# Giving each buffer that TensorE reads its own offset within 512 bytes, in a two-block float32 network

## The reference

```
_swiglu_ffn:  g, u = split(x @ w_gate_up);  (silu(g) * u) @ w_down        width 1024 -> 2 x 2816 -> 1024
conv_ffn:     u = causal_dwconv(x @ w_up);  (silu(gate) * up) @ w_down    width 1024 -> 2 x 2816 -> 1024
block 1:      u @ w_in,  mixed @ w_out,  h @ w_ple_gate,  two feed-forward nets per layer
block 2:      hn @ w_in,  mix @ w_out,  rmsnorm(h) @ w_ple_gate,  one feed-forward net per layer
```

## Time and profile before

| | before |
|---|---|
| time, median of 2 runs | 3952.97 us |
| span of the profiled execution | 3950.6 us |
| TensorE matmul busy | 3812.4 us (97%), 17790 matmuls |
| TensorE weight loads busy | 3050.4 us (77%) |
| VectorE / ScalarE / GpSimd busy | 2334.5 / 1510.9 / 511.5 us |
| mean granted TensorE clock | 0.986 |
| HBM read | 307.94 MB, 78 GB/s over the span |

### The profile page before, as it was taken

How to read it: one execution, slowest core, us unless ns; L and a number is a source line. 1 busy time by engine, 2 the same in 40 slices (tenths; PEclk the granted TensorE clock), 3 DMA queues, 4 the chain that set the end, 5 groups by cost and what they waited for, 6 DMA issues and landing times. The chain is left out here.

```text
span 3950.6 us, 46607 instructions
## 1 busy us (share of the span) xinstructions
PE 3812.4 (97%) x17790; PEld 3050.4 (77%) x17790; DVE 2334.5 (59%) x3213; ACT 1510.9 (38%) x2188; POOL 511.5 (13%) x366
## 2 busy tenths in 40 slices
PE   8999989999999998999989999999999999999997
PEld 6888758888788885788877678788877767878886
DVE  5455766445544475744467675775567665675656
ACT  3224653223322365322243444343343353343333
POOL 1001731000100055100020013200010002220002
PEclk9999989999999999999999999999999999999999
DMA  4333203333233330233332100122233110022222
GB/s 152 96 96 112 66 21 96 96 96 111 86 98 99 97 106 11 79 100 96 96 114 80 49 22 1 43 96 96 96 109 107 59 38 6 12 80 96 96 96 80
DMA packets 87018, 314.99 MB, mean 80 GB/s; under 512 B 10016, under 2 KB 10400, under 8 KB 86176
## 3 DMA queue, kind: packets, MB, share of 16 engines
q1 hardware_dynamic: 83664, 302.43, 24.4%
q10 hardware_dynamic: 3152, 9.74, 0.7%
HBM read 307.94 MB, written 2.10 MB: 78 GB/s over the span
## 5 line engine op out<-in xcount | busy, mean ns | idle before, releaser
L384 ACT ACTIVATE wh<-raw 128x1024 fp32r<-128x1024 f32 x564 | 597.4, 1059 | 1630.3 <-PE ps L404 1317.5
L402 PE MATMUL ps<-xh,wh 128*128 128x512 f32 x2336 | 918.0, 393 | 16.7 <-DVE xl L467 10.0
L403 PE MATMUL ps<-xl,wh 128*128 128x512 f32 x2336 | 910.8, 390 | 0.0
L404 PE MATMUL ps<-xh,wl 128*128 128x512 f32 x2336 | 910.5, 390 | 0.0
L388 DVE TENSOR_TENSOR wl<-raw,wh 128x1024 fp32r<-128x1024 f32 x564 | 695.6, 1233 | 181.1 <-ACT wh L384 180.2
L402 PEld LDWEIGHTS ps<-xh,wh 128*128 128x128 f32 x2336 | 439.8, 188 | 112.4 <-issue 19.6
L403 PEld LDWEIGHTS ps<-xl,wh 128*128 128x128 f32 x2336 | 440.0, 188 | 94.3 <-issue 3.6
L404 PEld LDWEIGHTS ps<-xh,wl 128*128 128x128 f32 x2336 | 439.8, 188 | 91.9
L402 PE MATMUL ps<-fh,wh 128*128 128x512 f32 x1016 | 397.1, 391 | 4.0 <-DVE wl L388 4.0
L404 PE MATMUL ps<-fh,wl 128*128 128x512 f32 x1016 | 395.4, 389 | 0.0
L403 PE MATMUL ps<-fl,wh 128*128 128x512 f32 x1016 | 395.3, 389 | 0.0
(11 more groups left out here) (467 smaller groups left out, 5529.6 us busy)
## 6 DMA issues: line engine op xcount, KB each, us to landing
raw<-in_w SPq DMA_DIRECT2D x564, 512.0 KB, 3.5
con<-in_consts SPq DMA_DIRECT2D x1, 2053.5 KB, 14.0
h<-in_x SPq DMA_DIRECT2D x4, 512.0 KB, 6.9
p_t<-in_p ACTq DMA_DIRECT2D x4, 512.0 KB, 3.9
w1k<-in_w1c ACTq DMA_DIRECT2D x2, 1024.0 KB, 4.9
w1v<-in_w1c ACTq DMA_DIRECT2D x2, 1024.0 KB, 7.0
out<-h SPq DMA_DIRECT2D x8, 256.0 KB, 2.2
dup_k<-roped ACTq DMA_DIRECT2D x8, 128.0 KB, 3.6
```

Source lines behind the costliest of these rows:

```text
L384: nc.scalar.activation(wh[k % 2][:, :], raw[k % 4][:, :], ACT.Copy).then_inc(s["w_hi"], 1)
L402: nc.tensor.matmul(DB[k % 2][:, :], a, hi(q), start=(q == order[0]), stop=False)
L403: nc.tensor.matmul(DB[k % 2][:, :], a, lo(q), start=False, stop=False)
L404: last = nc.tensor.matmul(DB[k % 2][:, :], b, hi(q), start=False, stop=(q == order[-1]))
```

## The change

The allocator gets a method `phase`, which moves the next start up to a given offset within 512 bytes. The buffers that TensorE reads in the dense stages get the phases of the table above. The skipped bytes need room, and it comes from a smaller scratch area for dynamic DMAs (4096 bytes per partition in place of the default; the first free byte falls from 16481 to 4193, so the arena starts at 4224 in place of 16512, and both have phase 128). Tensors that share the place of `fh` in the mixing stages (`qkv`, `roped`, `p_hi`, `p_lo`, `diag`, `sp_b`, `stick`, `w1k`, `w1v`, the accumulators `acc1` and `acc2`) move with it from phase 128 to 256; constants, `gbuf`, `sq`, `e_t`, `h` and all others keep their phase. No instruction is added, removed or moved on any engine.

```diff
+LINE = 512
@@ class Layout
+    def phase(self, offset):
+        self.at += (offset - self.at) % LINE
+        return self
@@ build
-        x_at = sb.at
-        xh = sb("xh", [P, DC, T], F32R)
-        xl = sb("xl", [P, DC, T], F32R)
-        f_at = sb.at
+        x_at = sb.phase(128).at
+        xh = sb.phase(128)("xh", [P, DC, T], F32R)
+        xl = sb.phase(160)("xl", [P, DC, T], F32R)
+        f_at = sb.phase(256).at
         fh = sb("fh", [P, 8, T], F32R)
-        fl = sb("fl", [P, 8, T], F32R)
+        fl = sb.phase(320)("fl", [P, 8, T], F32R)
+        sb.phase(128)
         raw = [sb(f"raw{k}", [P, UW]) for k in range(4)]
-        wh = [sb(f"wh{k}", [P, UW], F32R) for k in range(2)]
-        wl = [sb(f"wl{k}", [P, UW], F32R) for k in range(2)]
-        con_at = sb.at
+        wh = [sb.phase((128, 448)[k])(f"wh{k}", [P, UW], F32R) for k in range(2)]
+        wl = [sb.phase((160, 384)[k])(f"wl{k}", [P, UW], F32R) for k in range(2)]
+        con_at = sb.phase(128).at
@@ block1, block2
-                gl_ = Layout(nc, m.at, 32768)
-                gh, gl = (gl_(f"gate1{n}", [P, DC, T], F32R) for n in ("hi", "lo"))
+                gl_ = Layout(nc, m.at, 34816)
+                gh, gl = (gl_.phase(k)(f"gate1{n}", [P, DC, T], F32R) for n, k in (("hi", 32), ("lo", 416)))
...
+                gh, gl = (gl_.phase(k)(f"gate2{n}", [P, DC, T], F32R) for n, k in (("hi", 96), ("lo", 288)))
@@ kernel
-    nc = _bacc.Bacc("TRN2", target_bir_lowering=False, num_devices=1)
+    nc = _bacc.Bacc("TRN2", target_bir_lowering=False, num_devices=1, dynamic_dma_scratch_size=4096)
```

More of the change, by code:

```diff
@@ L1364, in block2 @@
                 m.at += -(-4 * NS2 // 32) * 32
-                gl_ = Layout(nc, m.at, 32768)
-                gh, gl = (gl_(f"gate2{n}", [P, DC, T], F32R) for n in ("hi", "lo"))
+                gl_ = Layout(nc, m.at, 34816)
+                gh, gl = (gl_.phase(k)(f"gate2{n}", [P, DC, T], F32R) for n, k in (("hi", 96), ("lo", 288)))
                 small_end = m.at
```

## The result

The changed kernel took 4011.36 us (two runs, 4011.27 and 4011.44) against 3952.97, +58.4 us, which is 1.0148 by the two medians. The ratio on record is 1.0143, with a 95% interval of 1.0123 to 1.0163: under two per cent, but clear of the noise. The forecast was 3928, range 3870 to 3995. The slower rival had said 4005.

What follows compares the result with a forecast made beforehand. The prediction took TensorE's matmul pitch in the dense stages as the bound. Its terms, 8.4 - 25.2 - 7.8 = -24.6 us from 3952.97, gave 3928 us, range 3870 to 3995.

Steps and rivals of the forecast that it cites:

- slower rival: Odd x and all f units: any distance other than 0 costs 6.4 ns, +52 us, 4005 us (half price 3979); chance 0.25.
- What bounds: Dense stages: TensorE is the bound, so each nanosecond between two matmuls counts; one nanosecond on all is 13 us.
- The scratch, ScalarE, VectorE: 0.: Whole kernel: smaller DMA scratch costs 0, and ScalarE and VectorE work at other phases is covered by their idle half.
- Moved tensors of the mixing stages, at 0: Mixing stages: moved tensors such as qkv cost 0, since TensorE reads them in short pieces between waits.
- `x`, even (4176 matmuls): Even units streaming x: stream-to-next-weights distances all stay 0, so no change, 0 us.
- The prediction's own sign of being wrong: Dense x units: if x even moves as much as x odd, distance within a pair is not what counts.
- I take the middle, 223 ns: Dense units at new distances: pitch assumed between no loss, 213 ns, and the gates' 233.1; with a duration reading, about 224.7.
- -25.2 us: Odd x, odd f and a third of even f units: -3.7 ns on each of 6800 matmuls.
- 224.4 in the middle: Dense units: alternative middle pitch using the skill's 215.7 ns as lower end in place of 213; sum -15 us.
- `f` even at +6.4 for its `fh` matmuls: Even f units: distance 128 for two of three matmuls, 1312 in all, costs 6.4 ns each, +8.4 us.
- the pairs: Dense units: each matmul's pitch priced by the distance between its stream and the next matmul's weights, within 512.
- No effect: Whole kernel: buffer place has nothing to do with the pitch; all stays at 3953 us, within 5 us; chance 0.16.

Runs made afterwards that it cites:

- first experiment: Against the kernel before the change: only the small DMA scratch, all buffers at their old phases; 3953.5 us against 3952.51, ratio 1.0008.
- the roles: Against the old-phase kernel with small scratch: xl to 160, odd wl to 160, gate1 to 128/192, gate2 to 128/128, so single buffers are off; 4009.02 us.

## Why the prediction was wrong

- **What bounds** held: TensorE's pitch, ns by ns. 58.6 of 58.9 us are in it.
- **The scratch, ScalarE, VectorE: 0.** Held (first experiment; busy times equal to 0.4 us). Moved tensors of the mixing stages, at 0: the rest is 0.8 us longer, clock included, and no run took them apart.
- **The step that failed: "`x`, even (4176 matmuls) ... All three as before. No change, 0 us."** It took the distance between a stream and the weights loaded beside it as what counts. The prediction's own sign of being wrong came true: `x` even moved nearly as much as `x` odd, 5.2 ns against 6.1. The even `x` units, at distance 0 in every pair, went from 227.1 to 232.3 and cost 20 us, the run with all lo buffers at 160 showed 232.1 with nothing but such pairs, and the roles showed that a single buffer off makes a neighbour late that reads none of it. As far as it was tried, what must agree is the whole set, hi, lo, `wh` and `wl`, modulo 256.
- **The second: "I take the middle, 223 ns".** It stood between 213, for which there was no row of these matmuls at full clock, and 233, for which there were two. Of the distances mapped, six of seven other than 0 are at 232.7 to 234.2 and one at 228.9; mixed sets are at 229.7 to 233.1 in the changed kernel, and at 229.0 to 234.1 in all. The single reading that pointed lower, a duration of 387 ns, is of a matmul whose whole set stood at 128, and says nothing of another distance. The rows of the gates were the nearest of their kind, and the price should have been theirs. -25.2 us would have been +44. (With 224.4 in the middle the same working gives -14, not the -15 that is written there.)
- **`f` even at +6.4 for its `fh` matmuls**: measured 229.7 for the unit, +2.9 on the mean, where the sum had (2 x 6.4 - 3.7) / 3 = +3.0. Right by luck, since single steps don't follow pairs: from a start on line 409, 410 and 411 to the next it is 226.2, 229.2 and 234.6 on the mean, where the pairs said 233, 223 and 233.
- **The slower rival** had place and price: 8112 matmuls at +6.4, +52 us. It left out `x` even (+20 us) and priced the others too high (they cost 38, `f` above all); the two errors nearly cancelled, 4005 against 4011, so its time is in part luck. "The pitch seems to have no reason to be best at 0" was the argument against it, and it was no reading of a row. Chance 0.25 was too little for the only case whose price was in the trace.
- **No effect** is refuted. The Trainium skill has TensorE's two read ports as independent, so that loading the next weights takes nothing from the running matmul ("TensorE: Matmul & The Clock Gate", "Step-by-step: what each phase is for"), and says that TensorE waits for nobody in SBUF ("SBUF — State Buffer", "Who interferes with whom"). The trace agrees that no other engine disturbs it, as far as it shows: over all `x` and `f` units before, whatever ScalarE and VectorE do beside, the mean pitch is 226.8 to 227.1. It speaks against it for TensorE's own reads: the same instructions stand at 226.7 or 233 by nothing but addresses, and moving only the lo weights by 32 bytes cost 6.2 ns a matmul. By what path the addresses act, no run shows.

## What to carry to other kernels

Buffers that feed one chain of float32r matmuls, streams and weights, should all start at the same offset modulo 256 bytes; packing them back to back in multiples of 256, as the kernel before does, gives it for nothing, and spreading them cost 1.4% here. When rows show one case at a good price and another at a bad one, and the change moves work from the first toward something unknown, price it at the bad row, not at a middle for which there is no row. And look at the granted clock of the short-matmul stages before crediting a few microseconds saved elsewhere.

## What the runs showed of the hardware

- Where TensorE's operands start matters, with a period of 256 bytes: 226.7 ns with all alike (at 128 and at 160), 228.9 at 64, up to 234.2 at 160 for a 512-column float32r matmul with its 128-column weight load. Differences of 32 bytes were the smallest tried. A single step can be shorter than 226.7 in a mixed set (the 226.2 above), the mean of a unit never was.
- At half clock the pitch is 426 ns, which is 512 columns at 1.2 GHz with one a cycle: no loss. The addresses don't matter there either. In the changed kernel an even unit on `x`, with lo off by 32, takes 1.28 us over three steps at a granted clock of 0.50, 427 ns each:

```profile
23.45 0.63 PE L410 MATMUL ps<-xl,wh 128*128 128x512 f32 x1
...
24.73 0.60 PE L410 MATMUL ps<-xl,wh 128*128 128x512 f32 x1
```

  Over all 34 such steps of `x` in that profile the mean is 426.7, as over the 31 before, and over 8 of odd units in the kernel with `f` and the gates put back it is 426.8. At full clock the even units are 5.2 ns slower than before, the odd ones 6.1.
- At full clock even the best set loses 13.6 ns a matmul against half of 426. What that remainder is stays open, as does the mechanism by which one buffer off delays two matmuls.
- A stretch of short matmuls can keep the full clock in one execution and get half of it for a time in another of nearly the same kernel (1.00 against 0.73 on the mean over the same 25 us), and each such fall, 13.7 us long, cost 4 us here. Two of them outweigh the 5 us that the edit had saved elsewhere.
